# A two-layer decoder trunk with expert retrieval: part of its first stage moved between TensorE, VectorE and GpSimd, two more weight slots, and later expert bookkeeping

## The chip, the cores and the metric

The kernel is one launch on one core of a Trainium2 chip (trn2), all in float32. The metric is the device time of the launch in microseconds (us): the median of several runs. A traced execution of its own gives the profile. In the text PE is TensorE, DVE is VectorE, ACT is ScalarE, POOL is GpSimd, SP is the sync engine; SP and POOL each issue DMAs, and all of these run on the core's 16 DMA engines.

## The reference, cut to what matters

256 tokens of width 1024 go through two layers. A layer turns the conditioning vector c into six modulation vectors ("ada" blocks of 1024 columns), does sparse attention and a causal 31-tap convolution over the projected input, and then, for each token, fetches 128 expert rows u, takes their dot products with the token, and sums 128 expert rows v with the results.

```python
for l in range(DEPTH):                                  # 2 layers
    mod = (silu(c) @ w_ada[l] + b_ada[l])[:, None, :]   # w_ada[l]: 1024 x 6144
    sh1, sc1, g1, sh2, sc2, g2 = split(mod, 6)
    h = rms_norm(x) * (1 + sc1) + sh1
    q, k, v, qi, ki, wi, cu = split(h @ w_in[l])
    attn = dsa_attention(norm_rope(q), norm_rope(k), v, rope(qi), norm_rope(ki), wi)
    conv = silu(layer_norm(depthwise_conv31(glu(cu)) + b))
    x = x + g1 * (concat(rms_norm(attn), rms_norm(conv)) @ w_out[l])
    h2 = rms_norm(x) * (1 + sc2) + sh2
    # per token: 8 heads x 2 halves of h2 @ w_q scored against 128 sub keys, top 16 of each half,
    # top 16 of their sums -> 8 x 16 = 128 expert numbers e and gates g
    x = x + g2 * sum_k(g_k * gelu(u[e_k] . h2) * v[e_k])   # u, v: 16384 rows of 1024 floats a layer
```

## The kernel before, in words

The 256 tokens are two tiles of 128, and there are two layers: four **parts**, p = 2 * layer + tile. Each part has a first half (projections, attention, convolution: `first`, `attend`) and a second half (output projection, h2, the choice of experts: `second`), then its expert rows are fetched: 128 u gathers and 128 v gathers, each one indirect DMA of 128 rows of 4 KB (512 KB), issued by POOL (L639 and L647). `rows` is a ring of 13 slots for these gathers. DVE takes a u row with one fused multiply and sum (`dots_to`, L1407); PE takes four v rows at a time (`v_to`, L833). While part p's rows arrive, PE, DVE and ACT work on part p+1. In part 0 there is nothing earlier to overlap with, so it runs at the head of the launch beside the weight loads alone.

**Order of the work.** `plan()` writes one list of weight blocks and of PSUM jobs. SP loads the blocks in that order, in pieces of 1 MB, into weight slots (`slot_of`), and waits, in that same order, until the piece that was in the slot has been used (`wait_weight_used`, L585 issues). PE walks the same list; a job takes the next of four PSUM banks (`RING = 4`) and waits until it is free. The slots are the four of `wring`, and at first also borrowed space: slots 4 to 6 are rows 6 to 11 of the gather ring, slots 7 and 8 are the tile `spread_c`, which is later cleared and used for the v sums (`FIRST_WSLOTS = 9`). From block ("wq", 0, 2) on only the four of `wring` are used.

**Modulation.** A product ("ada", l, j) is 16 matmul steps of PE (L716, 32 instructions), a copy by ACT to `stages`, and a turn ("adaT", l, j) by PE (L692 to L702) into columns or rows. Where each stands is the table `ADA`; for part 0 there are the places pre, preT, conv, convT, S, mix, out, wq1, wq2, tail. Product (0, 2) gives g1, and (0, 4) the scale of h2.

**Part 0, first half.** ACT writes h turned and scaled (L1118) from two ring banks; PE opens the ca/cg banks with zero products (L776) and projects (L788); DVE makes the gated input of the convolution (`glu`, L1477). The convolution of the 4 channel blocks is split: block 0 on PE with diagonal matrices that ACT builds (L1150, L814, two `conv` calls), blocks 1 and 2 on DVE as 62 tap instructions (L1529 to L1534, in groups by `TAP_STEPS`), block 3 on POOL (L623 to L627, 61 instructions). Then PE projects qi, ki, q, k, v (L730, L886), turns the sub keys (L678), DVE does the index norm, the index scores, the selection and the q/k norm (L1502 to L1507), then the logits (L1571), `conv_norm` (L1599) and `join` (L1612).

**Part 0, second half.** PE projects the output (L730), DVE adds it and makes h2 (L1716 to L1719), PE projects the queries of the experts (("wq", 0, b), L744), scores them (L1052), ACT copies both out, DVE chooses (`choose`, from L1617) and writes the expert numbers (`decode`, L1686). The first head's numbers (`head_ready`) let POOL issue its first gather. Between the four choices DVE does dots up to `FIRST_DOTS`. After the last it does the index and q/k norms of part 1, clears `spread_c` (L1744), and in `finish_choice` waits for the turned expert numbers (job "eT", which PE does after the modulation work of place "tail"), copies them for the v gathers (L1691), and normalizes the gates.

## Time and profile before

| | |
|---|---|
| median of 3 runs | 1772.59 us (1772.22 to 1772.85) |
| the profiled execution, its own time | 1771.43 us |
| its span in the trace | 1769.6 us |
| PE busy | 1020.7 us (58%) |
| DVE busy | 1079.7 us (61%) |
| POOL busy | 1017.6 us (58%) |
| ACT busy | 273.2 us (15%) |
| bytes moved by DMA | 693.85 MB, mean 392 GB/s |

The profile page divides the span into 40 equal slices of 44.2 us. A digit is a busy share in tenths, 9 standing for 90% or more; the GB/s line gives what the 16 DMA engines moved in each slice. A "chain of waits" is followed back from the last instruction: at each step to what released it. In tables by stretch, "DMA share" is the mean busy share of the 16 DMA engines, and a value a little above 1 means full.

### The profile page before, as it was taken

To read this page: it belongs to the slowest core of one execution; us is meant where nothing else is said; L and a number is where in the kernel's file an instruction comes from. 1 tells how busy PE (TensorE), PEld (TensorE's weight loads), DVE (VectorE), ACT (ScalarE), POOL (GpSimd) and SP (SyncE) were. 2 spreads that over 40 slices of the span, in tenths; PEclk is the share of its full clock that TensorE was granted. 3 is DMA by queue.
4 is the path that set the end of the run, shared out by engine and by line. 5 is a ranking of instruction groups with operands and counts; after the bars stand their busy time and mean duration, and the time that the engine had idled before them with its cause. 6 is when DMAs were issued, how large, how long until landed. Compare 5 with 4: busy or idle time off the path is not lost.

```text
span 1769.6 us, 17929 instructions
## 1 busy us (share of the span) xinstructions
PE 1020.7 (58%) x6037; PEld 564.8 (32%) x6037; DVE 1079.7 (61%) x2957; ACT 273.2 (15%) x741; POOL 1017.6 (58%) x1131
## 2 busy tenths in 40 slices
PE   4998996602798478620798568820679620004554
PEld 2655863400355156500246126610226300000111
DVE  1663999699316676779416656689622969991000
ACT  2231332300201024400100022510210100000000
POOL 2520453477664664466655674467665777776774
PEclk8998998655899889855699879965789865556888
DMA  9979999999999999999999999999999999999998
GB/s 352 322 281 343 363 402 406 350 409 410 407 403 404 408 407 397 385 410 410 406 366 409 409 409 405 405 393 410 409 409 404 409 399 410 410 409 390 409 410 336
DMA packets 199404, 693.85 MB, mean 392 GB/s; under 512 B 23942, under 2 KB 23958, under 8 KB 199314
## 3 DMA queue, kind: packets, MB, share of 16 engines
q0 software_dynamic: 147776, 537.19, 76.7%
q1 hardware_dynamic: 51538, 155.54, 23.1%
q8 instruction: 48, 0.79, 0.2%
q14 instruction: 42, 0.34, 0.1%
HBM read 691.60 MB, written 1.05 MB: 391 GB/s over the span
## 4 chain that ended last, share of the span: by engine, by line
DMA 37%; PE 28%; DVE 14%; POOL 13%; issue 6%; ACT 1%; SPq 0%; DVEq 0%; ACTq 0%; POOLq 0%
DMA rows<-in_peer_v,v_at 19%; DMA rows<-in_peer_u,u_at 14%; PE ps L833 7%; DVE rows L1407 7%; POOL rows L647 7%; POOL rows L639 6%; PE ps L788 6%; PE ps L760 3%; PE ps L730 2%; DMA wring<-in_w_in 2%; PE ps L814 2%; DMA spread_c<-in_w_ada 1%; PE ps L716 1%; PE ps L776 1%; DMA wring<-in_w_ada 1%
## 5 line engine op out<-in xcount | busy, mean ns | idle before, releaser
L639 POOL DMA_INDIRECT rows<-in_peer_u,u_at x512 | 482.6, 943 | 398.5 <-DVE dots L1407 215.8
L1407 DVE CUSTOM_DVE_ANT_0 rows<-rows,ps 128x1024 f32<-128x1024 f32 x512 | 608.8, 1219 | 78.5 <-DMA rows<-in_peer_u,u_at 64.9
L647 POOL DMA_INDIRECT rows<-in_peer_v,v_at x512 | 488.5, 954 | 282.1 <-PE ps L833 154.3
L833 PE MATMUL ps<-rows,spread_c 128*32 128x512 f32 x2048 | 322.4, 759 | 212.0 <-DMA rows<-in_peer_v,v_at 211.9
L678 PE MATMUL ps<-ident,coef 128*128 128x128 f32 x4 | 1.9, 476 | 403.9 <-DVE coef L1751 403.9
L833 PEld LDWEIGHTS ps<-rows,spread_c 128*32 128x32 f32 x2048 | 70.5, 127 | 410.7 <-issue 408.6
L788 PEld LDWEIGHTS ps<-hT,wring 128*128 128x128 f32 x1248 | 144.3, 195 | 25.1 <-issue 23.1
L788 PE MATMUL ps<-hT,wring 128*128 128x128 f32 x1248 | 149.5, 280 | 1.2 <-ACTq L1122 1.2
L678 PEld LDWEIGHTS ps<-ident,coef 128*128 128x128 f32 x4 | 0.7, 182 | 406.6 <-DVE coef L1751 406.6
L760 PE MATMUL ps<-wring,hT 128*128 128x512 f32 x256 | 121.6, 619 | 11.8 <-ACTq L1122 5.9
L1150 ACT ACTIVATE diag_eq<-ident,cwT 128x128 f32<-128x128 f32 x372 | 111.4, 387 | 36.0 <-PE ps L814 34.8
L814 PE MATMUL ps<-diag_eq,hc 128*128 128x128 f32 x744 | 103.1, 303 | 20.7 <-ACT diag_eq L1150 20.7
L814 PEld LDWEIGHTS ps<-diag_eq,hc 128*128 128x128 f32 x744 | 98.7, 216 | 27.6 <-ACT diag_eq L1150 25.7
L1420 DVE TENSOR_TENSOR gy<-ps,g 128x512 f32<-128x512 f32 x8 | 5.5, 689 | 162.0 <-PE ps L833 161.8
L1617 DVE MAX8 v<-mixed_use 128x8 f32<-128x128 f32 x64 | 15.6, 285 | 124.1 <-ACTq L1110 122.3
L760 PEld LDWEIGHTS ps<-wring,hT 128*128 128x128 f32 x256 | 47.8, 197 | 73.8 <-issue 56.2
L1107 ACT COPY mixed_use<-ps 128x512 f32<-128x512 f32 x52 | 30.4, 585 | 258.6 <-PE ps L788 147.3
L1344 ACT ACTIVATE dots<-dots 128x128 f32<-128x128 f32 x4 | 1.2, 309 | 418.5 <-DVE dots L1407 418.5
L1716 DVE TENSOR_TENSOR gy<-ps,g 128x512 f32<-128x512 f32 x8 | 5.5, 692 | 88.8 <-PE ps L760 74.2
L716 PE MATMUL ps<-wring,cact 128*32 128x512 f32 x240 | 36.7, 739 | 23.3 <-DMA wring<-in_w_ada 23.3
L1118 ACT ACTIVATE hT<-ps,modcol 128x128 f32<-128x128 f32 x60 | 22.5, 455 | 142.9 <-PE ps L678 141.9
L1407 DVE DVE_READ_ACCUMULATOR2_ANT dots<- 128x1 f32 x512 | 42.0, 82 | 0.0
(225 smaller groups left out, 1156.9 us busy)
## 6 DMA issues: line engine op xcount, KB each, us to landing
wring<-in_w_in SPq DMA_DIRECT2D x41, 1024.0 KB, 14.7
wring<-in_peer_wq SPq DMA_DIRECT2D x32, 1024.0 KB, 9.4
wring<-in_w_ada SPq DMA_DIRECT2D x30, 1024.0 KB, 9.9
rows<-in_w_ada SPq DMA_DIRECT2D x17, 1024.0 KB, 11.2
wring<-in_w_out SPq DMA_DIRECT2D x15, 1024.0 KB, 17.2
rows<-in_peer_u,u_at POOLq DMA_INDIRECT x512, 14.1
rows<-in_peer_v,v_at POOLq DMA_INDIRECT x512, 10.0
spread_c<-in_w_in SPq DMA_DIRECT2D x3, 1024.0 KB, 11.0
```

Of the source, the lines that this page charges most:

```text
L639: pool.indirect_dma_start(row(n), None, u_rows, bass.IndirectOffsetOnAxis(ap=u_at[:, p % 2, k:k + 1], axis=0)).then_inc(row_landed[n % SLO ...
L647: pool.indirect_dma_start(row(n), None, v_rows, bass.IndirectOffsetOnAxis(ap=v_at[:, p % 2, tok:tok + 1], axis=0)).then_inc(row_landed[n % ...
L716: ins = pe.matmul(o[32 * g:32 * g + 32, :], cact[:, k:k + 1].to_broadcast([P, 32]), ws[:, i, 512 * cc:512 * cc + 512], start=h == 0, stop= ...
L730: ins = pe.matmul(o, lhs[:, 4 * h + j, :], w[:, j, :], start=h + j == 0, stop=4 * h + j == 7)
L760: ins = pe.matmul(o, lhs[:, k, :], w[:, j, 512 * cc:512 * cc + 512], start=k == 0, stop=k == KT - 1)
L788: ins = pe.matmul(o[:, i * P:(i + 1) * P], w[:, j, at:at + P], rhs[:, k, :], start=False, stop=(k, i) == (KT - 1, 3))
L814: ins = pe.matmul(o[:, cols], hc[:, ct, t * P + i:t * P + i + P], tap_diag(p, n, i - i0), start=False, stop=i == TAPS - 1)
L833: ins = pe.matmul(ps[32 * g:32 * g + 32, YB + q, :], spread_c[:, g, a, :], row(n)[:, q * 512:q * 512 + 512], start=a == 0, stop=a == 31)
L1107: act.copy(dst, o if src is None else src(o)).then_inc(free[b], 1)
L1118: ins = act.activation(hT[:, k, :], o[:, i * P:(i + 1) * P], ACT.Identity, bias=0.0 if shift is None else shift[:, k:k + 1], scale=scale[: ...
L1150: ins = act.activation(tap_diag(p, n, i - i0), ident[:, :], ACT.Copy, scale=cwT[:, ct, i:i + 1])
L1407: dve.tensor_tensor_reduce(out=row(n), in0=row(n), in1=h2_shown, scale=1.0, scalar=0.0, op0=ALU.mult, op1=ALU.add, accum_out=dots[:, k:k + ...
```

## The change

It does eight things, all in part 0 but for the last of them:

- The products of modulation blocks (0, 2) and (0, 4) leave PE. Their pieces become blocks "adav"; DVE multiplies each of the 8 slices of 128 x 1024 by a column of silu(c) and adds (`ada_product`), the sum staying in rows 12 and 4; PE sums over partitions with a column of ones in the turn. Semaphore `ada_taken` frees the pieces. (0, 2) is done before `glu(0)`, (0, 4) between the mixed columns and the output product.
- Convolution block 0 moves from PE and ACT to DVE: 93 tap instructions instead of 62, the last 26 of them after the logits. The transposes of all 4 blocks come behind those of the attention weights.
- The turned h of part 0 goes to banks 4 and 5, outside the ring.
- The sub keys are loaded and turned later, after the attention values.
- `FIRST_WSLOTS` is 11: rows 0 to 3 are slots 7 and 8, `spread_c` slots 9 and 10. From ("wq", 0, 1) on seven slots are used, from ("wq", 0, 2) on four.
- The first expert query block is done by head (`proj_heads`): the first head's scores are computed three quarters through it.
- The norms of part 1 move from between the choices to behind 20 and 44 further dots; `finish_choice(0)` moves behind dot 100; `spread_c` is cleared by POOL before its gather 96.
- In `V_GROUPS` the v groups of tile 0 (part 2) are spread a little differently.

```diff
-FIRST_WSLOTS = 9
+FIRST_WSLOTS = 11
...
-TAP_STEPS = (24, 18)
-V_GROUPS = [((4, 6), 7, (8, 9, 10), 11), ((4, 5, 6, 7), 9, (10, 11, 12), 13)]
+TAP_STEPS = (24, 18, 25)
+V_GROUPS = [((4, 7), 8, (9, 10, 11), 12), ((4, 5, 6, 7), 9, (10, 11, 12), 13)]
 
...
+VEC_ADA = ((0, 2), (0, 4))
 
 ADA = {
     (0, "pre"): [product(0, 0), product(0, 1)],
...
-    (0, "convT"): [turn(1, 0)],
-    (0, "S"): [product(0, 2), product(1, 1), turn(0, 2), turn(1, 1)],
-    (0, "mix"): [product(0, 3)],
-    (0, "out"): [turn(0, 3), product(0, 4), turn(0, 4)],
+    (0, "S"): [product(1, 1), turn(1, 0), turn(1, 1)],
+    (0, "mix"): [turn(0, 2), product(0, 3)],
+    (0, "out"): [turn(0, 3), turn(0, 4)],
...
+WIDE = ("ada", "adav", "wqs", "outs", "cacg", "vqi", "qk")
...
-        if p != 1:
+        if p > 1:
             for q in range(2):
                 job("hT", p, q)
         ada(p, "preT")
         if p == 0:
             both("cacg", p)
+            block("adav", 0, 2)
...
-            for name in ("k", "v", "sk"):
+            for name in ("k", "v"):
                 both(name, p)
             ada(p, "conv")
-            ada(p, "convT")
             job("qT", p)
             job("kT", p)
...
         if p == 0:
+            both("sk", p)
             ada(p, "mix")
...
-            for b in range(2):
-                both("out", p, b)
+            both("out", p, 0)
+            block("adav", 0, 4)
+            both("out", p, 1)
             ada(p, "out")
...
     n_first = use_at[(("wq", 0, 2), 0)]
+    n_low = use_at[(("wq", 0, 1), 0)]
     KEPT = (FIRST_WSLOTS - 2, FIRST_WSLOTS - 1)
     slot_of, use_before, held = [], [], {}
...
+            top = WSLOTS if i >= n_first else WSLOTS + 3 if i >= n_low else KEPT[0] if i >= FIRST_WSLOTS else FIRST_WSLOTS
+            slot = next(s for s in order if s < top)
         order.remove(slot)
...
-            half = spread_c[:, 2 * (slot - WSLOTS - 3):2 * (slot - WSLOTS - 3) + 2, :, :]
+            if slot < WSLOTS + 5:
+                at = 2 * (slot - WSLOTS - 3)
+                return rows[:, at:at + 2, :].rearrange("p s n -> p (s n)")
+            half = spread_c[:, 2 * (slot - WSLOTS - 5):2 * (slot - WSLOTS - 5) + 2, :, :]
             return half.rearrange("p g a c -> p (g a c)")
...
+            if uses[i] in vec_count:
+                eng.wait_ge(ada_taken, vec_count[uses[i]])
+            elif uses[i] in piece_count:
                 eng.wait_ge(piece_used, piece_count[uses[i]])
...
-            if 6 <= n < 12:
-                slot = WSLOTS + (n - 6) // 2
+            if n < 4 or 6 <= n < 12:
+                slot = WSLOTS + (3 + n // 2 if n < 4 else (n - 6) // 2)
...
-            if p == 0:
-                return rows[:, n, j * P:(j + 1) * P]
...
+        vec_sum = {(0, 2): rows[:, 12, :], (0, 4): rows[:, 4, :]}
...
+                    if (p, k) == (0, 96):
+                        b, used = bank(("v", 1))
+                        pool.wait_ge(full[b], used)
+                        pool.memset(spread_c[:, :, :, :].rearrange("p g a c -> p (g a c)"), 0.0).then_inc(spread_cleared, 1)
...
+                        vec = (l, j) in VEC_ADA
+                        if vec:
+                            pe.wait_ge(ada_taken, vec_count[("adav", l, j), 3])
+                        else:
+                            st = stages[:, stage_at[(l, j)] % 2, :]
+                            pe.wait_ge(stage_ready, stage_at[(l, j)] + 1)
...
+                        elif vec:
+                            pe.wait_ge(bcol_ready, 1)
+                            b, o = open_job("adaT", l, j)
+                            pe.matmul(o[:, 0:8], ident[:, :], bcol[:, 6 * l + j, :, :].rearrange("p q c -> p (q c)"),
+                                      start=True, stop=False)
+                            for i in range(8):
+                                at = 2 * (i % 4) + i // 4
+                                ins = pe.matmul(o[:, at:at + 1], vec_sum[l, j][:, i * P:(i + 1) * P], ones[:, :],
+                                                start=False, stop=i == 7)
+                            ins.then_inc(full[b], 1)
...
+            def proj_heads(block, rhs, between):
+
+                w = [piece(block, 0), piece(block, 1)]
+                for c, name in enumerate(jobs_of(block)):
+                    b, o = open_job(*name)
+                    for i in range(2):
+                        for k in range(KT):
+                            at = (2 * c + i) * P
+                            ins = pe.matmul(o[:, i * P:(i + 1) * P], w[k // 4][:, k % 4, at:at + P], rhs[:, k, :],
+                                            start=k == 0, stop=k == KT - 1)
+                            if (c, i, k) == (1, 1, 3):
+                                ins.then_inc(piece_used, 1)
+                        if (c, i) == (1, 0):
+                            between()
+                    ins.then_inc(full[b], 1)
...
+                if p == 0:
+                    for k in range(KT):
+                        ins = pe.transpose(ps[:, HB + k // 4, (k % 4) * P:(k % 4 + 1) * P],
+                                           hb[:, k * P:(k + 1) * P], ident[:, :])
+                        if k % 4 == 3:
+                            ins.then_inc(h0_full, 1)
+                    return
...
+                    next_is("block", ("adav", 0, 2))
...
                     proj(("v", p), hT)
-                    subkey_turns()
                     ada(p, "conv")
-                    conv(p, 0)
-                    conv(p, 1)
-                    ada(p, "convT")
                     pe.wait_ge(qk_ready, p + 1)
...
-                    pe.wait_ge(conv_dve, 2)
-                    pe.wait_ge(conv_pool, 1)
-                    pe.wait_ge(diag_used, 4)
-                    for ct in range(1, CT):
-                        ins = pe.transpose(ps[:, CONV_BANK, ct * P:(ct + 1) * P], acc[:, ct, :], ident[:, :])
-                    ins.then_inc(conv_full, 1)
                     ada(p, "S")
                     pe.wait_ge(proj_ready, 5)
                     for n in ns:
                         pe.wait_ge(exp_ready, n + 1)
                         turn4(("PT", l, n), [ex[:, n % 2, j * P:(j + 1) * P] for j in range(4)])
+                    pe.wait_ge(conv_dve, CT - 1)
+                    pe.wait_ge(conv_pool, 1)
+                    for ct in range(CT):
+                        ins = pe.transpose(ps[:, CONV_BANK, ct * P:(ct + 1) * P], acc[:, ct, :], ident[:, :])
+                    ins.then_inc(conv_full, 1)
                     for n in ns:
                         values(p, n)
+                    subkey_turns()
                     ada(p, "mix")
...
-                    for b in range(2):
-                        proj(("out", p, b), hT)
+                    proj(("out", p, 0), hT)
+                    next_is("block", ("adav", 0, 4))
+                    proj(("out", p, 1), hT)
                     ada(p, "out")
...
-                    for b_ in range(4):
+                    proj_heads(("wq", p, 0), hT, lambda: subkeys(0, 0))
+                    show_h2()
+                    subkeys(0, 1)
+                    for b_ in range(1, 4):
                         proj_turned(("wq", p, b_), ("qp", p, b_), hT)
-                        if b_ == 0:
-                            show_h2()
                         subkeys(b_)
                         if b_ in (1, 2):
                             ada(p, f"wq{b_}")
...
+                if p == 0:
+                    for k in range(KT):
+                        if k % 4 == 0:
+                            act.wait_ge(h0_full, k // 4 + 1)
+                        ins = act.activation(hT[:, k, :], ps[:, HB + k // 4, (k % 4) * P:(k % 4 + 1) * P], ACT.Identity,
+                                             bias=modcol[:, l, 0, k:k + 1], scale=modcol[:, l, 1, k:k + 1])
+                        if k % 4 == 3:
+                            ins.then_inc(hT_ready, 1)
+                    return
...
                 if p == 0:
-                    make_diags(p, 0, 1, 2, 3)
...
+            def ada_product(l, j):
+
+                o = vec_sum[l, j]
+                for h in range(4):
+                    i = use_at[(("adav", l, j), h)]
+                    dve.wait_ge(w_landed[slot_of[i]], 16 * use_number[i])
+                    w = weight_slot(slot_of[i]).rearrange("p (k n) -> p k n", k=2)
+                    if h == 0:
+                        seq_(ts(o, w[:, 0, :], cact[:, 0:1], None, ALU.mult))
+                    else:
+                        seq_(stt(o, w[:, 0, :], cact[:, 2 * h:2 * h + 1], o, ALU.mult, ALU.add))
+                    seq_(stt(o, w[:, 1, :], cact[:, 2 * h + 1:2 * h + 2], o, ALU.mult, ALU.add), ada_taken)
+
+            tap_steps = [(i, ct) for i in range(TAPS) for ct in range(CT - 1)]
+
+            def taps(n):
+
+                for i, ct in tap_steps[:n]:
+                    o, w = acc[:, ct, :], cwT[:, ct, i:i + 1]
...
+                if p == 1:
+                    more_dots(20)
+                    index_norms(p)
+                    more_dots(24)
+                    qk_norms(p)
                 if p > 1:
                     more_dots(16)
                     glu(p)
                     more_dots(14)
                 elif p == 0:
+                    dve.wait_ge(cact_made, 1)
+                    ada_product(0, 2)
                     glu(p)
                     dve.wait_ge(cw_ready, 1)
                     taps(TAP_STEPS[0])
@@ -1554,7 +1651,7 @@
                 if p != 1:
                     qk_norms(p)
                 if p == 0:
-                    taps(len(tap_steps))
...
                     logits(n)
+                if p == 0:
+                    taps(len(tap_steps))
                 conv_norm(p)
...
-                if h0 == 0:
-                    dve.wait_ge(s_ready, 4 * p + blk + 1)
+                dve.wait_ge(s_ready, scored(p, blk, h1 - 1))
...
                     dve.sem_inc(mixedT_ready, 1)
+                    ada_product(0, 4)
                 dve.wait_ge(g1_ready, 2 * (l + 1))
...
                     if p == 0:
                         if blk == 2:
                             glu(1)
-                        elif blk == 3:
-                            index_norms(1)
                         dots_to(0, FIRST_DOTS[blk])
-                if p == 0:
-                    qk_norms(1)
-                    wait_full(dve, ("v", 1))
-                    seq_(dve.memset(spread_c[:, :, :, :].rearrange("p g a c -> p (g a c)"), 0.0))
-                finish_choice(p)
+                if p:
+                    finish_choice(p)
 
             def coefficients(p):
+                if p == 0:
+                    dots_to(p, 100)
+                    finish_choice(p)
                 dots_to(p, P)
...
                 if p:
                     dve.wait_ge(v_used, p * P)
+                else:
+                    dve.wait_ge(spread_cleared, 1)
```

## Rows read from the trace of the kernel before

**Rows 1.** The page, the span in 40 equal slices: GB/s moved.
```profile
GB/s 352 322 281 343 363 402 406 350 409 410 407 403 404 408 407 397 385 410 410 406 366 409 409 409 405 405 393 410 409 409 404 409 399 410 410 409 390 409 410 336
```
**Rows 2.** Table by stretch: stretch, length, engines' busy us, PE clock granted, DMA share, GB/s.
```profile
0.00:188.00 188.00, 155.17 (x897) 96.90 (x901) 84.74 (x286) 43.90 (x118) 46.56 (x108) 0.90 0.88 321
188.00:326.00 138.00, 113.07 (x662) 78.25 (x655) 118.12 (x402) 41.02 (x121) 55.89 (x59) 0.87 1.03 403
326.00:337.00 11.00, 7.11 (x40) 6.29 (x38) 9.64 (x19) 9.48 (x29) 5.54 (x6) 0.63 0.58 194
337.00:1755.00 1418.00, 740.14 (x4412) 382.14 (x4412) 864.40 (x2248) 178.80 (x475) 909.61 (x960) 0.76 1.02 404
1755.00:1769.60 14.60, 5.18 (x32) 1.18 (x32) 2.76 (x4) 0.00 (x0) 0.05 (x1) 0.82 0.48 188
```
**Rows 3.** Timeline of POOL, 185 to 330 us: start, us, instruction, [idle before, releaser].
```profile
187.96 1.10 POOL L639 DMA_INDIRECT rows<-in_peer_u,u_at  x1 [84.65 <-DVE u_at L1686]
...
329.93 0.94 POOL L639 DMA_INDIRECT rows<-in_peer_u,u_at  x1 [27.23 <-DVE dots L1407]
```
**Rows 4.** Timeline of DVE, 268 to 345 us.
```profile
309.03 3.47 DVE L1744 MEMSET spread_c<- 128x4096 f32 x1 [0.92 <-DVE pj L1435]
326.11 0.29 DVE L1691 CAST v_at<-ps 128x128 uint32<-128x128 f32 x1 [13.61 <-PE ps L678]
```
**Rows 5.** Timeline of SP, 0 to 200 us: weight loads issued.
```profile
174.60 14.87 SPq L585 DMA_DIRECT2D wring<-in_peer_wq  x4
```
**Rows 6.** Chain of waits, 36 to 200 us: start, us, what.
```profile
39.48 3.75 PE ps L776 x4
...
92.68 1.75 PE ps L678 x16
...
98.41 7.12 PE ps L814 x62
...
112.17 8.74 PE ps L716 x64
...
139.38 15.77 PE ps L730 x32
...
156.15 3.61 PE ps L716 x32
...
164.36 10.21 PE ps L744 x64
```
**Rows 7.** Timeline of DVE, 0 to 215 us.
```profile
60.44 0.69 DVE L1477 TENSOR_TENSOR hc<-ps,mixed_use 128x512 f32<-128x512 f32 x1 [35.24 <-ACT mixed_use L1165]
...
61.88 7.45 DVE L1531 SCALAR_TENSOR_TENSOR rows<-hc,cwT,rows 128x128 f32<-128x128 f32 x22
...
96.22 1.23 DVE L1505 TENSOR_TENSOR pj<-pj,rs 128x1024 f32<-128x1024 f32 x1
...
100.32 5.50 DVE L1531 SCALAR_TENSOR_TENSOR rows<-hc,cwT,rows 128x128 f32<-128x128 f32 x18
...
110.42 0.69 DVE L1571 TENSOR_TENSOR mixed_use<-ps,bias 128x512 f32<-128x512 f32 x1 [3.77 <-PE ps L847]
...
113.73 0.70 DVE L1599 BATCH_NORM_STATS2 bn<-ps 128x6 f32<-128x512 f32 x1
...
177.22 0.49 DVE L1617 MAX8 v<-mixed_use 128x8 f32<-128x128 f32 x2 [9.23 <-ACTq L1110]
```
**Rows 8.** Timeline of PE, 0 to 200 us.
```profile
59.56 3.60 PE L730 MATMUL ps<-wring,hT 128*128 128x512 f32 x8
...
136.08 1.95 PE L678 MATMUL ps<-ident,hb 128*128 128x128 f32 x8 [3.10 <-DVE hb L1612]
139.38 5.47 PE L730 MATMUL ps<-rows,hT 128*128 128x512 f32 x8 [1.35 <-DVEq L1710]
```
**Rows 9.** Timeline of POOL, 0 to 65 us.
```profile
8.06 0.21 POOL L607 MEMSET tri<- 128x128 f32 x1
...
61.41 0.48 POOL L623 TENSOR_SCALAR rows<-hc,cwT 128x128 f32<-128x128 f32 x1 [47.62 <-DVEq L1478]
```

88 lines of the change are left out of this document (48 added, 40 removed).

## The prediction

> **What bounds the kernel now.** I read the page's slices first [rows 1]: from the tenth slice on the DMA engines move 400 to 410 GB/s almost without a break, whatever engine is busy. I take 410 as the full rate, so a 512 KB row (0.524 MB) costs 1.28 us. Where the rate is lower, DMA time is lost. The table by stretch [rows 2] says where. Bytes are the rate times the length. Up to 188 us: 321 x 188 = 60.3 MB, 147.2 us at the full rate, so 40.8 us are lost. From 188 to 326: 403 GB/s, little. From 326 to 337: 194 GB/s, or 2.1 MB in 11 us, 5.8 us lost. From 337 to 1755: 404, an average of small losses that the change hardly touches. The last 14.6 us are the tail. The change doesn't alter the bytes. So the end moves by what these losses move, and engine time counts only where it makes the DMA engines idle.
>
> Two events set the losses. The **first gather** starts at 187.96 after POOL waited 84.7 us for DVE's expert numbers [rows 3]. Before it only weights can be moved, and only as far ahead as the slots reach. The **stall at 326**: DVE stands 13.61 us in `finish_choice` for the turned expert numbers [rows 4]; no dot frees a row, POOL issues nothing for 27.2 us [rows 3], the queued transfers run dry.
>
> **The path to the first gather, step by step.** The chain of waits [rows 6] is mostly PE, with DVE in between.
>
> 1. Zero products. L776 starts at 39.48, after the copies of h have freed the ring's banks. With h outside the ring it runs beside them, and the projection L788 starts at about 39.5 instead of 43.2: **-3.7 us**. The matrices for convolution block 0 leave ACT, which was early anyway: nothing.
> 2. Product (0, 2) on DVE before `glu`. Eight instructions, the nearest rows being a two-input instruction of 1024 at 1.23 us [rows 7]: 9.8 us. DVE is idle for 35.2 us there [rows 7]. What it waits for are pieces 12 to 15 of the load order. 12 pieces, x and the small loads are 13.4 MB; the rate reaches 350 GB/s over the first 40 us (14 MB), so piece 15 lands near 49 and the sum is ready near 51, before the gate at 56.7. Cost nothing; queued behind it are `glu`, and through `glu` POOL's taps. Without the cover each us of lateness would cost one us.
> 3. From 60.44 to the end of the q/k norm at 100.3 DVE has no idle time, so the block keeps its length and ends at 96.6. Then 25 taps, the logits, 26 taps. Taps come every 0.306 us at 100 us (18 in 5.50) and every 0.339 beside POOL's taps (22 in 7.45) [rows 7]; I take 0.33, and 0.30 to 0.60 as bounds, the far one because a 128-column instruction of POOL takes 0.48 [rows 9] and two may get in each other's way. 51 taps: 16.8 us, logits 3.3: 116.7. Before, `conv_norm` began at 113.73 [rows 7]; now four transposes and it begins at 117.3: **+3.6**. But it no longer waits for values afterwards. Before, from L1599 it took 4.9 us, then waited until 129.5; mixed columns were ready at 136.0. Now: 117.3 + 4.9 + 6.5 (join) = **128.7**.
> 4. PE meanwhile. Saved: 7.12 of convolution (L814), half of L716's 8.74 at 112, all of 3.61 at 156 [rows 6]. Moved: the sub-key turns, 1.75 [rows 6], now behind the values, with the sub-key load moved past 12 pieces in SP's order; it lands near 98, used at 119. After the transposes: values 2.0, sub keys 1.75, turn (0, 2) 4.2, product (0, 3) 3.7: 129.0 with a warm PE. Waits before qT and before the transposes (3 to 4 us each) put 1 us on it: **130.0**, a little after DVE. So the mixed columns' transposes start at 130.0 against 136.08 [rows 8]: **-6.1**.
> 5. Output product 15.77 us, 3.3 us after that start: 133.3 to 149.1. DVE's product (0, 4), again 9.8 us, ends near 142, before the second half of the output is there at 149; SP's order reaches its pieces 42 and 43 by 128. Nothing. Pieces 42 and 48 to 51 now wait for the sub keys and for DVE instead of PE; some 3 us of DMA idle near 120, inside the loss counted below.
> 6. From the end of the output product (155.15) to L744 (164.36) h2 took 9.2 us [rows 6], with the 3.61 us product and its turn in front of PE's transposes. Without them about 1.4 less: L744 at **156.9** against 164.36.
> 7. By head. From L744 to DVE's first choice took 12.9 us (164.36 to 177.22 [rows 6, 7]). Now half a block 5.8 (PE is cold there), a quarter 1.9, scores and copies 1.2: 8.9, **-4.0**. First choice at 165.8, first gather at **176.6**, 11.4 us earlier.
>
> Clock of PE: after a wait the first 8 instructions of the output product took 5.47 us, in a stretch with 1.35 to 3.10 us of idle before, against 3.60 for the same 8 in a busy stretch [rows 8]. The chain in step 4 stands between these. The Trainium skill, "TensorE: Matmul & The Clock Gate", section "What's actually happening", says that the slow clock is the default and activity releases it, which speaks against taking work off PE. By that rule all of step 4's 12 us could run slow and its 1 us would be up to 12.
>
> **From the first gather to the bytes.** The load order before 176.6 reaches the second piece of ("ada", 1, 3)'s end (54 pieces), since ("wq", 0, 2) waits for ("wq", 0, 1), used near 175. Before, two of L744's pieces more had gone by 188 [rows 5]. So 60.3 - 2.4 = 57.9 MB are moved, 141.2 us at the full rate; the first row's bytes start 1 us after issue, 177.6. Lost: 36.4, against 40.8: **-4.4 us**. This is the step where most of the 11.4 us goes: the DMA engines stand idle from about 155 to 177. The two added slots help the start but close at ("wq", 0, 1), and no slot can hold ("wq", 0, 2).
>
> **The stall at 326.** `finish_choice` now comes behind dot 100, near 365 us, when "eT" has long been done; dots run on, one in 1.14 us against a row in 1.28. **-5.8 us**. Its cover: the 8.6 us of q/k norm after dot 90 stop the dots, but 13 rows (16.6 us) are out. DVE's clearing, 3.47 us [rows 4], goes to POOL in front of gather 96. POOL's memset of 128 columns took 0.21 [rows 9]; by columns that is 6.7 us for 4096, and by its 0.48 us instruction of 128 columns [rows 9] 15 us. I take 4, near DVE's; transfers take 8 to 10 us to land there, so nothing is lost. POOL's pitch (1.24 us a gather) hardly catches up, so over 9 us it would lose.
>
> `V_GROUPS`: same work, nothing; at most 1 us either way.
>
> **Sum.** -4.4 - 5.8 = -10.2 against the profiled execution's 1771.43 us (span 1769.6 and 1.8 around it): 1761.2, and the median of the runs is 1.2 us above it. I give **1761 us**.
>
> **The rivals.**
> - *Only one of the two comes off* (chance 0.20). A cold PE or slower taps put 4 to 5 us on steps 3 and 4, so the first gather comes at 181 and the start gives nothing; or the clearing and the norms together starve the rows and the stall comes back smaller. 1771.4 - 5.8 = **1766**. For: idle of PE before each cold stretch [rows 8]. Against: PE has less to do in just these places.
> - *The start gives more* (0.17). PE stays warm through the output product and L744, some 2 + 2 + 1.5 us, and all that is earlier than 176.6 counts in full, since no more bytes are possible: 1761 - 5.5 = **1755.5**.
> - *The change doesn't do what it says*: the first gather moves but the DMA engines idle just as long, because the weights that fill the time are held by slots and the stall only moves to the v rows (0.05): **1770**.
> - *DVE becomes the bound* (0.05), the other side. Place: the 51 taps between the q/k norm and `conv_norm`, on the path one for one. At 0.60 us each they cost 30.6 us instead of 16.8: the first gather at 190.4, lost 191.4 - 141.2 = 50.2, +9.4 - 5.8: **1775**. It decides from a pitch of 0.53 us (+10.2). Against it: 0.31 to 0.34 in three groups. The Trainium skill, "SBUF — State Buffer", section "Who interferes with whom", says that a DVE instruction with two SBUF inputs and a GpSimd instruction that reads SBUF block each other fully; taps on both are just that. The trace agrees mildly (0.339 beside POOL, 0.306 mostly after it).
>
> **How the numbers follow.** The forecast has 0.53 (1758 to 1764). A measurement here can tell about 0.2%, 3.5 us: faster means under 1769.0. The forecast, the first rival and the second lie there; of these I keep back 0.02 for the first rival's upper end: faster 0.88. Same: the third rival, those 0.02 and 0.01 of the fourth that falls short of its price: 0.08. Slower: the rest of the fourth, 0.04. For 8 in 10 the range takes the forecast, the second rival and most of the first: 1752 to 1768.
>
> **What would show it.** The first gather (L639 of before) near 176.6; L744 near 157; `conv_norm` near 117; tap pitch under 0.35; no DVE wait over 3 us between 260 and 400; DMA rate near zero between 155 and 176, and 400 GB/s or more from there to 400. Wrong if a wait for piece 15 stands before `glu`, if POOL's taps end after 116, or if a gap of DMA appears behind gather 96 or at the turn from u to v rows.

## The result, and the profile after

Five runs of each kernel: 1772.85 us before and 1762.39 us after (1759.50 to 1766.24), a ratio of 0.9948, 95% interval 0.9932 to 0.9963. It is faster by more than 0.2%, and the forecast of 1761 us was 1.4 us under the median. The profiled execution took 1759.5 us, the lowest of its five, with a span of 1757.2 us. So its 12.4 us of difference in span are on the large side for a median difference of 10.5.

The page's GB/s line, to be held against [rows 1]: the second and third slice (44 to 132 us) rose, the fourth (132 to 176) fell, the eighth (308 to 351) lost its dip, and the ninth (351 to 395) has a new one.

```profile
PE 1020.7 (58%) x5918; PEld 566.7 (32%) x5918; DVE 1104.3 (63%) x3003; ACT 262.9 (15%) x710; POOL 1021.9 (58%) x1132
...
GB/s 351 389 346 249 405 402 409 409 380 409 393 409 401 409 409 395 396 410 410 406 368 408 409 406 404 409 409 409 404 385 408 400 411 410 409 410 404 409 409 325
```

DVE's 24.6 us more work and ACT's 10 us less move nothing by themselves. The table by stretch, columns as in [rows 2]. It ends where the last 14.6 us begin, as the fourth row does there:

```profile
0.00:188.00 188.00, 148.76 (x826) 97.25 (x827) 125.00 (x409) 34.24 (x88) 57.94 (x119) 0.89 0.91 338
...
326.00:337.00 11.00, 2.05 (x7) 1.43 (x7) 9.03 (x29) 2.55 (x9) 3.73 (x4) 0.50 1.03 410
337.00:1742.60 1405.60, 753.71 (x4444) 390.76 (x4444) 854.64 (x2239) 184.46 (x495) 898.91 (x944) 0.76 1.02 404
...
155.00:176.00 21.00, 20.28 (x166) 18.98 (x168) 14.28 (x80) 2.66 (x6) 2.02 (x2) 0.91 0.25 88
...
360.00:400.00 40.00, 7.82 (x24) 5.62 (x24) 39.01 (x76) 4.23 (x6) 25.83 (x28) 0.50 0.99 377
```

The stall at 326 is gone: 410 GB/s where there were 194. Between 155 and 176 us the DMA engines stand almost still (88 GB/s), as forecast. Between 360 and 400 they lose 40 x (1 - 377/410) = 3.2 us, which was not forecast; the kernel before lost none there.

The timeline of DVE and of POOL, in the places of [rows 7], [rows 4] and [rows 3]:

```profile
44.39 0.75 DVE L1480 TENSOR_SCALAR rows<-wring,cact 128x1024 f32<-128x1024 f32 x1 [19.11 <-DMA wring<-in_w_ada]
...
53.53 1.28 DVE L1483 SCALAR_TENSOR_TENSOR rows<-rows,cact 128x1024 f32<-128x1024 f32 x1
55.65 0.69 DVE L1582 TENSOR_TENSOR hc<-ps,mixed_use 128x512 f32<-128x512 f32 x1 [0.83 <-ACT mixed_use L1240]
...
57.34 7.07 DVE L1494 SCALAR_TENSOR_TENSOR rows<-hc,cwT,rows 128x128 f32<-128x128 f32 x21
...
94.73 7.63 DVE L1494 SCALAR_TENSOR_TENSOR rows<-hc,cwT,rows 128x128 f32<-128x128 f32 x25
...
105.57 6.13 DVE L1494 SCALAR_TENSOR_TENSOR rows<-hc,cwT,rows 128x128 f32<-128x128 f32 x23
114.24 0.70 DVE L1698 BATCH_NORM_STATS2 bn<-ps 128x6 f32<-128x512 f32 x1 [1.30 <-PE ps L1053]
...
162.96 0.49 DVE L1716 MAX8 v<-mixed_use 128x8 f32<-128x128 f32 x2 [5.31 <-ACTq L1176]
...
382.78 0.29 DVE L1789 CAST v_at<-ps 128x128 uint32<-128x128 f32 x1
```

```profile
173.67 1.10 POOL L667 DMA_INDIRECT rows<-in_peer_u,u_at  x1 [74.62 <-DVE u_at L1784]
...
355.49 3.53 POOL L664 MEMSET spread_c<- 128x4096 f32 x1
...
372.86 0.94 POOL L667 DMA_INDIRECT rows<-in_peer_u,u_at  x1 [4.51 <-DVE dots L1512]
```

`v_at` is copied without a wait where there were 13.61 us of one. The 4.51 us in the last row are POOL waiting for a dot: they stand behind the q/k norm of part 1, in which DVE does no dot. PE, in the places of [rows 6] and [rows 8]:

```profile
34.70 2.50 PE L836 MATMUL ps<-brow,ident 24*128 24x512 f32 x4
38.13 6.08 PE L848 MATMUL ps<-hT,rows 128*128 128x128 f32 x32 [0.94 <-ACT hT L1226]
...
112.99 1.11 PE L1053 MATMUL ps<-ident,rows 128*128 128x128 f32 x4 [2.65 <-DVE rows L1497]
113.90 3.52 PE L918 MATMUL ps<-vals,mixed_use 128*128 128x64 f32 x16
117.20 3.62 PE L706 MATMUL ps<-ident,wring 128*128 128x128 f32 x16
...
128.82 1.09 PE L706 MATMUL ps<-ident,hb 128*128 128x128 f32 x8
131.26 14.00 PE L774 MATMUL ps<-rows,hT 128*128 128x512 f32 x32 [1.35 <-DVEq L1808]
...
150.43 1.97 PE L706 MATMUL ps<-ident,hb 128*128 128x128 f32 x8 [2.15 <-DVE hb L1818]
154.02 6.16 PE L802 MATMUL ps<-hT,rows 128*128 128x128 f32 x32 [1.62 <-DVEq L1828]
```

### The profile page after: what moved, and what is told of

The parts are those of the page before. It is cut to its first block, busy times and chain, and to the rows that moved or that the text cites. A ratio compares the mean times of both kernels' runs of the same rounds, so it can differ in the third digit from the quotient of the medians.

```text
span 1757.2 us, 17710 instructions
## 1 busy us (share of the span) xinstructions
PE 1020.7 (58%) x5918; PEld 566.7 (32%) x5918; DVE 1104.3 (63%) x3003; ACT 262.9 (15%) x710; POOL 1021.9 (58%) x1132
## 4 chain that ended last, share of the span: by engine, by line
DMA 38%; PE 24%; DVE 15%; POOL 14%; issue 7%; ACT 1%; SPq 0%; POOLq 0%; DVEq 0%; ACTq 0%
DMA rows<-in_peer_v,v_at 18%; DMA rows<-in_peer_u,u_at 17%; PE ps L893 8%; DVE rows L1512 7%; POOL rows L667 7%; POOL rows L675 7%; PE ps L848 6%; DMA wring<-in_w_in 2%; PE ps L820 2%; DVE rows L1494 2%; PE ps L788 1%; DMA rows<-in_w_ada 1%; PE ps L836 1%; PE ps L706 1%; PE ps L774 1%
## 5 line engine op out<-in xcount | busy, mean ns | idle before, releaser
L893 PEld LDWEIGHTS ps<-rows,spread_c 128*32 128x32 f32 x2048 | 70.4, 126 | 399.1 <-issue 396.7
L1173 ACT COPY mixed_use<-ps 128x512 f32<-128x512 f32 (+1 forms) x54 | 30.7, 569 | 300.9 <-PE ps L848 142.4
L760 PE MATMUL ps<-wring,cact 128*32 128x512 f32 x208 | 32.1, 744 | 23.4 <-DMA wring<-in_w_ada 23.4
## 6 DMA issues: line engine op xcount, KB each, us to landing
rows<-in_w_ada SPq DMA_DIRECT2D x15, 1024.0 KB, 17.5
```

Source lines behind the costliest of these rows:

```text
L760: ins = pe.matmul(o[32 * g:32 * g + 32, :], cact[:, k:k + 1].to_broadcast([P, 32]), ws[:, i, 512 * cc:512 * cc + 512], start=h == 0, stop= ...
L893: ins = pe.matmul(ps[32 * g:32 * g + 32, YB + q, :], spread_c[:, g, a, :], row(n)[:, q * 512:q * 512 + 512], start=a == 0, stop=a == 31)
L1173: act.copy(dst, o if src is None else src(o)).then_inc(free[b], 1)
```

## The experiments

**How they are read.** Timed comparisons are against the kernel before on the same chip. For each profile I also summed the DMA time lost, by the prediction's method: length x (1 - rate/410) over windows of 20 to 60 us of the table by stretch. The totals differ from that of the kernel before as the spans do, to within 0.8 us (before 76.9, after 64.5: 12.4 us, and so the spans). The total takes in the time from 1740 us on as well, 8 to 10 us in every kernel. From 480 to 1740 us the loss lies anywhere between 14 and 23 us; no run tells why, and it is as large a spread as the effects looked for. The profiled executions aren't always typical: that of `tail_alone` was the fastest of its twelve (1765.2 us), that of `norms_early` the slowest of its six (1764.94 us). "Gather" is the start of the first gather, "query" that of the first query matmul (L802 of the changed kernel).

| kernel | ratio [interval] | query | gather | lost 0-200 | 200-360 | 360-480 | 480-1740 | total |
|---|---|---|---|---|---|---|---|---|
| before | 1 | 164.36 | 187.96 | 41.8 | 8.1 | 0.2 | 18.9 | 76.9 |
| after | 0.9948 [0.9932, 0.9963] | 154.02 | 173.67 | 33.1 | 1.2 | 5.2 | 16.0 | 64.5 |
| control | 0.9943 [0.9930, 0.9956] | 156.73 | 177.01 | 36.3 | 1.2 | 5.5 | 18.0 | 69.5 |
| tail_back | 0.9997 [0.9988, 1.0006] | 155.43 | 174.10 | 33.5 | 13.9 | 0.1 | 17.5 | 74.1 |
| tail_alone | 0.9987 [0.9975, 0.9998] | 164.31 | 186.73 | 40.5 | 1.3 | 6.1 | 14.3 | 70.7 |
| clear45 | 0.9943 [0.9929, 0.9957] | 155.64 | 175.29 | 34.5 | 1.2 | 5.0 | 17.6 | 66.7 |
| norms_early | 0.9934 [0.9920, 0.9948] | 158.44 | 178.73 | 38.0 | 1.4 | 1.7 | 21.4 | 70.8 |
| slots12 | 0.9937 [0.9924, 0.9950] | 153.77 | 173.31 | 30.6 | 1.2 | 6.5 | 17.4 | 64.4 |
| best2 | 0.9924 [0.9908, 0.9941] | 155.02 | 174.65 | 31.8 | 1.4 | 0.7 | 22.8 | 65.8 |
| no_heads | 0.9961 [0.9950, 0.9972] | 155.32 | 178.37 | 34.4 | 1.1 | 9.1 | 16.8 | 70.0 |
| slots9 | 0.9952 [0.9936, 0.9969] | 159.24 | 178.34 | 34.9 | 1.2 | 6.2 | 17.7 | 68.6 |
| ada4_pe | 0.9943 [0.9927, 0.9960] | 155.24 | 175.30 | 34.7 | 1.2 | 4.9 | 18.0 | 67.1 |
| taps62 | one run, 1754.51 us | 148.72 | 168.26 | 27.6 | 1.1 | 6.1 | 15.4 | 60.4 |
| ring_h | one run, 1764.7 us | 160.08 | 179.47 | 38.8 | 1.2 | 5.9 | 15.7 | 70.4 |

**The changed kernel once more.** No edit.

> The changed kernel as it is, beside the others on the same chip. Theory: 10 to 13 us faster than before (ratio 0.993 to 0.994); first gather at 173.7 us, DMA rate near 0 from 160 to 170 us, and small holes (320 to 370 GB/s in 5 us stretches) between 370 and 400 us.

1761.37 us against 1771.04, 9.7 us faster. But its first gather came 3.3 us later than in the profile above, from the same code. The earliest difference is the clock of PE: between 27 and 33 us the granted clock was 0.50 here and 1.00 in the profile above, and it differs again near 125. The zero products took 2.77 us instead of 2.50, and the mixed columns' transposes began at 131.53 instead of 128.82. Five of the kernels below run the same code up to the first gather (after, control, tail_back, clear45, norms_early), and theirs lies anywhere from 173.67 to 178.73. So a single profile's first gather is good to some 5 us, the gain is read from the timed ratio, and a profile is read for its mechanism.

**The two halves of the change apart.** `tail_back` is the changed kernel with the bookkeeping of the choice as before:

```diff
+                        elif blk == 3:
+                            index_norms(1)
...
-                if p:
-                    finish_choice(p)
+                if p == 0:
+                    qk_norms(1)
+                    wait_full(dve, ("v", 1))
+                    seq_(dve.memset(spread_c ...))
+                finish_choice(p)
```

> Norms of part 1, clearing of spread_c and finish_choice put back where they were before (DVE clears). Theory: the stall comes back, DVE waits over 10 us for the turned expert numbers near 312 to 325 us and the DMA engines lose about 5.8 us there, while the holes at 370 to 400 us (3.2 us) go: 2 to 6 us slower than control. Rival: the moved bookkeeping gained nothing beyond what the new holes took: within 1 us of control.

The whole gain is gone: 0.9997, although the first gather stands at 174.10, 13.9 us earlier than before. That is some 9 us against the control, more than the 2 to 6 expected. The trace says where it went. DVE's timeline, PE's, and POOL's:

```profile
297.96 3.47 DVE L1834 MEMSET spread_c<- 128x4096 f32 x1 [0.92 <-DVE pj L1536]
...
323.72 0.29 DVE L1780 CAST v_at<-ps 128x128 uint32<-128x128 f32 x1 [22.29 <-PE ps L702]
```

```profile
311.43 1.94 PE L756 MATMUL ps<-wring,cact 128*32 128x512 f32 x8 [1.73 <-DMA wring<-in_w_ada]
...
323.16 0.45 PE L702 MATMUL ps<-ident,expert 128*128 128x128 f32 x1
```

```profile
327.54 0.94 POOL L663 DMA_INDIRECT rows<-in_peer_u,u_at  x1 [35.92 <-DVE dots L1508]
```

DVE reaches its wait 11 us earlier (301.4 instead of 312.5), but the turned expert numbers come when they came before (323.7 instead of 326.1), because PE's modulation products in front of them wait for their weights. So the wait grew from 13.61 to 22.29 us, POOL's pause from 27.2 to 35.9 us, and the loss from 200 to 360 us from 8.1 to 13.9 us. `tail_alone` is the kernel before with that same block of edits turned the other way, and nothing else:

> The kernel before with only the bookkeeping moved: norms of part 1 behind 20 and 44 further dots, clearing by POOL before gather 96, finish_choice behind dot 100. Theory (start and stall are coupled through the turned expert numbers, which come near 324 us whatever the start does): the stall's 6.5 us go, holes of about 3 us appear near 380 us, the start's 41 us of loss stay: 2 to 5 us faster than before, and together with the start alone (0 to 1 us) less than the whole (10 us). Rival (the two parts simply add): 8 to 9 us faster, the whole less what the start alone gave.

0.9987, 2.3 us. Its stall is gone as well (1.3 us lost), but 5.9 us come back as new holes from 360 to 480 us. So by the ratios the halves give 0.5 and 2.3 us alone and about 10 us together. The upper ends of their two intervals (2.1 and 4.4 us) still add up to less than the whole. The prediction added -4.4 and -5.8 as if each stood alone. They don't. An earlier start alone gained 8.3 us until 200 us and lost 5.8 of them in the longer wait. The moved bookkeeping alone took 6.8 us off the stall and lost 5.9 in new holes. An early start becomes worth its time when the wait is out of the way.

**What makes the new holes.** POOL's clearing (3.53 us in front of gather 96, over at 359.0) and DVE's q/k norm (8.8 us behind dot 90, from 362.6) are close together. `clear45` moves the clearing alone, from gather 96 to gather 45:

> POOL clears spread_c before gather 45 of part 0 instead of 96, where it stands idle for about 13 us waiting for dots. Theory (POOL's 3.53 us of clearing right before the 8.8 us pause of the dots is what empties the queue of rows): holes at 370 to 400 us shrink from 3.2 to under 1 us, 2 to 3 us faster than control. Rival (the pause alone empties the queue): no change, within 0.5 us.

Time (0.9943) and holes (5.0 us) stay: the rival holds. Without the clearing in between, the trace also shows the cover at work. POOL's timeline, the bytes that POOL's queue has moved from the first gather to 366.3 us and to 374 us (packets, MB, share of 16 engines), and two stretches of the table:

```profile
364.91 1.38 POOL L667 DMA_INDIRECT rows<-in_peer_u,u_at  x1 [0.30 <-issue]
374.47 0.94 POOL L667 DMA_INDIRECT rows<-in_peer_u,u_at  x1 [8.19 <-DVE dots L1512]
```

```profile
q0 software_dynamic: 13718, 49.99, 65.9%
q0 software_dynamic: 14584, 53.14, 67.3%
```

```profile
364.00:374.00 10.00, 1.01 (x4) 0.72 (x4) 9.35 (x22) 0.00 (x0) 1.98 (x2) 0.50 1.03 410
374.00:382.00 8.00, 0.11 (x1) 0.00 (x0) 8.00 (x15) 0.59 (x1) 5.64 (x6) 0.50 0.92 324
```

At 366.3 us the ring is full: 103 gathers issued, 90 dots done, 13 slots taken. But a taken slot isn't a row on its way. 49.99 MB are 95.3 rows of 0.524 MB, so 7.7 rows were on their way (9.8 us of bytes), and the other 5 had landed and waited for their dots. POOL stands for 8.19 us. At 374 us 53.14 MB are 101.4 rows: 1.6 rows are left, and there the rate falls to 324 GB/s. POOL then issues at its pitch of 1.24 us, hardly faster than a row moves (1.28), so the queue stays that thin and the holes go on behind 382 us. With the clearing in front of gather 96 nothing is different: POOL's two stops are 3.53 and 4.51 us there, 8.0 together, against 8.19 here.

`norms_early` leaves the clearing and moves the two norms of part 1 back, the index norm to behind block 3's dots and the q/k norm right behind the choices:

```diff
-                if p == 1:
-                    more_dots(20)
-                    index_norms(p)
-                    more_dots(24)
-                    qk_norms(p)
```

> Changed kernel with the index norm and the q/k norm of part 1 back between and right behind the choices, finish_choice and clearing left late. Theory (the holes of 3.3 us at 360 to 400 us come from the 8.8 us pause of the dots at a time when no weights are left to fill the queue; near 285 us the weight pieces fill it): loss from 360 to 400 us under 1 us, nothing new near 285 to 320, 2 to 3 us faster than control. Rival (any pause costs, wherever it stands): the holes move to 290 to 330 us, no gain.

The table by stretch has no hole from 360 to 400:

```profile
360.00:400.00 40.00, 6.70 (x20) 4.90 (x20) 38.64 (x69) 3.65 (x5) 30.98 (x32) 0.50 1.03 410
860.00:900.00 40.00, 30.01 (x132) 11.50 (x125) 6.20 (x22) 2.29 (x8) 21.75 (x23) 0.83 0.88 334
```

So it is the pause of the dots at this place that makes the holes, and the clearing isn't needed for them. The pause is as long where it stands now (POOL waits 6.95 us until 300.8), and it thins POOL's queue to 3.4 rows: 59 issued, 29.16 MB moved by 300 us. But SP's weights fill the engines beside it, and the rate from 290 to 304 us is 407 to 410 GB/s. That is the theory of the expectation. The time, though, fell by only 0.0009 against the control, within the intervals, where 2 to 3 us were expected. In this profile, the slowest of its six executions, more is lost later (21.4 us from 480 to 1740, against 16.0 to 18.0), for one between 860 and 900 us, where POOL waits for PE to use v rows (334 GB/s here, 342 in the control, 360 after and 359 before). Why these later holes differ was not tried.

**A twelfth slot.** `slots12` adds one weight slot, in the tile `diag_eq`, which part 0 no longer uses, and lets the first piece of ("wq", 0, 2) into a borrowed slot:

```diff
-FIRST_WSLOTS = 11
+FIRST_WSLOTS = 12
...
-    n_first = use_at[(("wq", 0, 2), 0)]
+    n_first = use_at[(("wq", 0, 2), 0)] + 1
+    n_diag = use_at[(("wq", 0, 3), 0)]
...
-            slot = next(s for s in order if s < top)
+            slot = next(s for s in order if s < top or s == WSLOTS + 5 and i < n_diag)
```

> One more weight slot in the tile diag_eq (free in part 0 now), and the first piece of query block (wq, 0, 2) allowed in rows 10 and 11. Theory (the DMA engines idle from 155 to 173 us for want of slots, 2.56 us a piece): two pieces more are moved before the first gather, 61 MB by 176 us instead of 58.7, 5 us faster than control. Rival (bytes moved early are given back, since DMA is not the bound behind the first gather, or gathers 10 and 11 wait for rows): 0 to 1 us.

Its first gather is where the changed kernel's is (173.31 against 173.67), and 2.5 us less are lost before it: about one piece of 1 MB (2.56 us at 410 GB/s), not the two expected. Of that 1 us shows in the time (0.9937 against 0.9943), inside the intervals, and so near the rival's 0 to 1 us. `best2` puts it together with `norms_early`:

> slots12 and norms_early together. If both are right: start loss near 31 us, 360 to 400 us under 1 us, 1755 to 1758 us, ratio to before 0.991 to 0.993. If gains at the start are given back later: like norms_early.

1759.07 us, 0.9924: the fastest version that computes the reference, 3.4 us under the control by the ratios (0.0019), with overlapping intervals.

**Is time at the start worth its length?** `taps62` leaves out convolution block 0 of part 0 (the block takes block 1's sums), so DVE has 31 taps less and the output is not the reference's:

```diff
-            tap_steps = [(i, ct) for i in range(TAPS) for ct in range(CT - 1)]
+            tap_steps = [(i, ct) for i in range(TAPS) for ct in (1, 2)]
```

> Changed kernel with convolution block 0 of part 0 left out (its channels get block 1's sums): 31 taps less on DVE, none on PE. Theory (PE's work before the mixed columns, subkey turns, turn (0, 2) and product (0, 3), ends just behind DVE's): conv_norm starts 9 us earlier, but the mixed transposes only 3 to 5 us earlier, and the first gather as much. Rival (DVE alone is the path): the whole 9 us.

The first gather comes 5.4 us before the changed kernel's, which is itself the earliest of the others with these loads, and 5.5 us less are lost by 200 us (27.6 against 33.1). Not all of it is the taps'. `conv_norm` begins at 111.98, 2.3 us earlier and not the 9 expected, since DVE first waits 5.26 us for PE there. And PE was granted the higher of its clocks (1.00) for the values and the sub keys, which took 2.00 and 1.92 us; in the changed kernel it was 0.50 there, and they took 3.52 and 3.62. So neither side of the expectation holds as it was put.

In the eight kernels with these same loads (after, control, tail_back, clear45, norms_early, ada4_pe, taps62, ring_h) gather + 1 - loss is 141.6 to 141.8 us: the bytes that can be moved before the DMA engines are busy again, at the full rate. The prediction had 141.2. But it isn't the gather that ends their idle time. In the changed kernel the load of ("wq", 0, 2) goes out at 171.80 us, the gather at 173.67, and the first packet of a row moves at 178.1, when the engines are already full again:

```profile
174.00:176.00 2.00, 2.00 (x21) 0.89 (x24) 1.90 (x15) 0.58 (x1) 1.70 (x2) 1.00 1.03 398
```

The sum is constant because in all eight that load goes out 1.9 us before the gather.

**The choice by head, the slots, the product (0, 4) and h outside the ring, undone one at a time.** The other parts of the change were not undone: product (0, 2) and convolution block 0 on DVE, the later sub keys, and `V_GROUPS`, which the prediction gave up to 1 us either way.

```diff
no_heads:
-        return [("qp",) + name[1:] + (c,) for c in range(2)] if name[1:] == (0, 0) else [("qp",) + name[1:]]
+        return [("qp",) + name[1:]]
```

> The changed kernel with the first query block of part 0 in one piece again, and with it its scores and its first choice, as before. By the prediction's step on the choice by head the stretch from the first query matmul (output wq of part 0, block 0) to the first gather goes back from 19.65 us to about 23.6 us (the kernel before had 23.60, the changed one 19.65, the control the same within 1 us), the first gather of this profile comes near 178 to 181, and the loss of DMA rate in the first 200 us grows by about 4 us. The time then stands about 3 to 4 us above the control's, ratio near 0.996 to 0.997. Rival: the choice by head is hidden, since the gathers behind the first are held by VectorE's choices and not by their own start; then the interval grows, the loss stays within 1 us of the changed kernel's and the ratio stays at 0.994.

From query to gather it takes 23.05 us, against 19.65 and 20.28 with the choice by head: the 3 to 4 us are real, and the gather comes at 178.37. But the loss until 200 us is 34.4, inside the 33.1 to 36.3 with it. The timeline of SP tells why. In the changed kernel, then in this one, the first load after the pause:

```profile
171.80 5.02 SPq L609 DMA_DIRECT2D wring<-in_peer_wq  x4
```

```profile
173.18 5.02 SPq L609 DMA_DIRECT2D wring<-in_peer_wq  x4
```

That is 17.8 and 17.9 us after the query's start: it is released when PE is through with ("wq", 0, 1), and the choice by head doesn't move it. It goes out 1.9 us before the first gather; 5.2 us before it here. A gather some 3 us later finds the engines busy with weights. So the choice by head moves a gather that for the moment is not what ends the idle time. Its time (0.9961, against 0.9943 of `ada4_pe` and 0.9952 of `slots9`, timed beside it) rather says that it is worth 1.6 to 3.2 us, with 9.1 us lost between 360 and 480 as the only larger sum; the intervals overlap and this stays open.

```diff
slots9:
-FIRST_WSLOTS = 11
+FIRST_WSLOTS = 9
```

> The changed kernel with nine first weight slots as before instead of eleven. Between 155 and 176 us the queue of weights has moved what it may, so two slots of 0.5 MB each less are 1.05 MB less ahead of the choices, 2.6 us at 410 GB/s. If the two slots carry their bytes' worth, the loss in the first 200 us grows by 2 to 3 us and the time stands 2 to 3 us above the control's, ratio near 0.9955. Rival: the two slots only fill earlier what is read later, and the second gate of VectorE's and PE's stage holds the rest; then the loss grows by under 1 us and the ratio stays within 0.0005 of the control's 0.9943. The run with a twelfth slot (0.9937) speaks weakly for the first.

```profile
67.29 5.40 PE L771 MATMUL ps<-wring,hT 128*128 128x512 f32 x8 [2.88 <-DMA wring<-in_w_in]
...
143.35 7.13 PE L771 MATMUL ps<-rows,hT 128*128 128x512 f32 x16 [0.89 <-DMA rows<-in_w_out]
...
159.24 5.93 PE L799 MATMUL ps<-hT,wring 128*128 128x128 f32 x35 [1.62 <-DVEq L1825]
```

```profile
168.89 14.31 SPq L606 DMA_DIRECT2D wring<-in_peer_wq  x4
```

With nine slots PE waits for weights at 67 us (2.88 us) and in the output product (0.89 us; first fence, PE), and the query starts at 159.24. But the query's weights lie in `wring`, not in borrowed rows, so the loads of ("wq", 0, 2) (second fence, SP) go out 9.7 us after the query instead of 17.8. Gather + 1 - loss is 144.4 instead of 141.6: 2.8 us more bytes before the gather, which makes up for much of its lateness. The expectation put a slot at 0.5 MB. A slot holds a piece of 1 MB, so the two are 5.1 us of bytes, and the loss until 200 us (34.9) isn't above that with eleven (33.1 to 36.3). The slots are worth less than their bytes; 0.9952 against 0.9943 doesn't decide between nothing and 3 us.

```diff
ada4_pe:
-    (0, "out"): [turn(0, 3), turn(0, 4)],
+    (0, "out"): [turn(0, 3), product(0, 4), turn(0, 4)],
```

> The changed kernel with the modulation product (0,4) back on TensorE behind the output product, product (0,2) stays on VectorE. By the prediction's sixth step the product leaving is worth 1.4 us from the output product to wq (the whole product is 3.6 us at the slower clock and 1.9 to 2.5 at the faster). So wq starts 1.4 to 3.6 us later than in the changed kernel (154.0 to 156.7 in the two profiles there are), and the time stands 1 to 3 us above the control's. Rival: the product hides in the gap before the transposes of h2 (2.15 us of waiting in the changed kernel), then wq starts within 1 us of it and the time is the control's.

PE's timeline of it, to be held against that of the changed kernel:

```profile
146.96 1.92 PE L759 MATMUL ps<-wring,cact 128*32 128x512 f32 x16
148.70 1.90 PE L759 MATMUL ps<-rows,cact 128*32 128x512 f32 x16
...
152.55 1.07 PE L705 MATMUL ps<-ident,hb 128*128 128x128 f32 x8
155.24 8.35 PE L801 MATMUL ps<-hT,rows 128*128 128x128 f32 x48 [1.62 <-DVEq L1825]
```

The product's 3.8 us fill what is a wait without it (2.15 us before the transposes of h2), and those transposes then run in 1.07 us instead of 1.97. From the output product's end to the query it takes 155.24 - 146.02 = 9.2 us, as it did before, against 154.02 - 145.26 = 8.8 us. Taking the product off PE gave 0.4 us there, and the time didn't move (0.9943). The rival of the expectation holds.

`ring_h` sends the transposes of the first h through the ring of banks again:

```diff
ring_h:
-        if p > 1:
+        if p != 1:
```

> The changed kernel with the transposes of the first normalised block through the ring of PSUM evacuations again, as before. By the prediction's first step the zero products are what came off, not the transposes' way, so the projection starts within 1 us of the changed kernel's 38.1 us if nothing in the ring stands ahead of it, and the time stays within 1.5 us of the changed kernel's. Rival: the ring's order holds the transposes behind the first modulation product's evacuation; then the projection starts near 41 to 43 us and conv_norm comes up to 3 us later (the time too).

```profile
34.11 1.84 PE L746 MATMUL ps<-halves,stages 128*128 128x2 f32 x8
...
41.78 3.75 PE L836 MATMUL ps<-brow,ident 24*128 24x512 f32 x4 [3.69 <-ACT hT L1177]
45.46 5.21 PE L848 MATMUL ps<-hT,rows 128*128 128x128 f32 x32
```

The projection starts at 45.46 instead of 38.13 us. 3.69 us of it are the zero products' wait for the ring's banks; most of the other 3.6 are PE's instructions at the lower clock (1.84 for 1.03, 3.75 for 2.50), which the control, with the same code as the changed kernel, had in part as well. The transposes themselves started at 32.06 without a wait for the ring. So it is not the wait that the expectation's rival named, but its size is near, and the prediction's first step had the right one: the zero products stand behind the copies of h. The first gather is at 179.47, 0.7 us above `norms_early`'s, and the one time there is, 1764.7 us, lies above the changed kernel's; a single run can't size it.

## Why the prediction was right, and where its steps were not

**The result** came out by the mechanism named (idle DMA engines at the start and at 326), but the two terms of the sum are not what they stood for, and that the time was met to 1.4 us is in part luck.

- *Step 1, zero products beside the copies of h.* Projection at 38.13, forecast 39.5, and `ring_h` shows that this edit does it.
- *Step 2, product (0, 2) on DVE.* It ran from 44.39 to 54.81 (1.28 us an instruction, not 1.23) and `glu` then waited 0.83 us for ACT, not for DVE. Nothing, as forecast; ready at 54.8, not 51, so 0.8 us were left of the cover.
- *Step 3, taps.* 0.337 us each beside POOL's taps (7.07/21), 0.305 in the group that begins beside them (7.63/25), 0.267 behind the logits, when POOL is done (6.13/23). So taps on both engines cost DVE a quarter more here, and the pitch stayed far from the fourth rival's 0.60. Forecast 0.33. `conv_norm` began at 114.24, forecast 117.3.
- *Step 4, PE.* The mixed transposes began at 128.82 (131.5 in the control), forecast 130.0. The clock did more than the prediction put 1 us on: after 2.65 us of waiting the granted clock was 0.50 from 113 to 120.7 us, and values and sub keys ran 3.52 and 3.62 us for 16 instructions each, where the sub keys before took 1.75 [rows 6]. That is some 3.4 us more. What made up for it is that the transposes and the values behind them began 3.4 us earlier than in the sum (113.90 against 117.3), since the taps were faster and the q/k norm ended sooner. DVE had the mixed columns ready at 126.4; PE's products ended last. The Trainium skill, "TensorE: Matmul & The Clock Gate", section "What's actually happening", has activity as what releases the slow clock. The trace agrees here and in `ada4_pe`: the transposes of h2 took 1.97 us behind a wait and 1.07 behind work. But the 12 us that step 4 might have lost by it were not seen; 3.4 us were.
- *Step 5.* The output product took 14.00 us, warm, not 15.77. DMA lost 5.6 us between 120 and 140 (8.2 in the control), forecast 3.
- *Step 6.* Query at 154.02 (156.73 in the control), forecast 156.9. The 1.4 us from the product's leaving were 0.4.
- *Step 7, by head.* -3.95 us (23.60 to 19.65), forecast -4.0. Right for the gather; `no_heads` shows no loss of DMA time that goes with it.
- *From the gather to the bytes.* The number is right to 0.6 us in eight kernels, but by a coincidence: the step has the first row end the idle time, and it is the load of ("wq", 0, 2), which goes out 1.9 us before the gather. Nor does a row move 1 us after its issue: the first packet came 1.8 us behind it before and 4.4 after. With the gather at 173.67 instead of 176.6 the start gave 8.7 us in the profile after and 5.5 in the control's; forecast 4.4. Of the 5.5 us more of the second rival ("the start gives more", PE warm) the profile after shows 4.3 and the control's 1.1.
- *The stall.* -6.4 us (6.5 to 0.1 from 320 to 360), forecast -5.8. Clearing on POOL 3.53 us, forecast 4, and nothing lost by it (`clear45`).
- **The step that failed** is the cover of the q/k norm: "13 rows (16.6 us) are out". It took slots for rows on their way. In `clear45` 13 slots were taken when POOL stopped, but only 7.7 rows (9.8 us) were on their way; 8.19 us later 1.6 were left, the rate fell to 324 GB/s, and POOL's pitch of 1.24 us could not thicken the queue again. So 3.3 us were lost from 360 to 400 and 1.9 more until 480, where before lost 0.2. The prediction's own sign of being wrong, a gap behind gather 96, had come up. The first rival said that the norms and the clearing together might starve the rows. The norms alone did; what came back, 5.0 us, is near the 5.8 of the stall, but at another place.
- **And the sum's form failed.** The halves alone give 0.5 and 2.3 us, not 4.4 and 5.8. Together they give about 10. The prediction treated the stall as a constant of 5.8 us, but it grows with the distance between DVE's arrival and a time that the start hardly moves. The total came out because errors offset: a start 1 to 4 us better than forecast and 1 us more from 200 to 360, against 5.0 us of new holes. These windows alone give 10.6 us for the profile after and 7.1 for the control's; the rest of the difference in their spans lies behind 480 us, where no step looks.
- *The chances.* The fourth rival's price, 1775, is within the 3.5 us that the prediction calls the same, so its 0.04 for slower doesn't follow from it.

## What to carry to other kernels

When an early stage is shortened, look for the next wait on something that doesn't move with it (here PE's turned numbers, held by weight loads): much of what was gained goes into that wait (5.8 of 8.3 us here), and only both edits together pay, so that undoing either one seems to prove that it was everything. A ring's slots aren't its cover. Of 13 taken slots only 7.7 held rows on their way, the others landed ones that waited for DVE, and a pause of 8.19 us used up nearly all of them; so compare a pause with what is issued and not yet moved. Where issue and transfer have nearly the same pitch (1.24 and 1.28 us) the queue doesn't thicken again. The same pause cost nothing where weights filled the engines beside it. And if two releases end an idle time within a few us of each other (a load and a gather), moving one of them is worth little.
